# First loads cut and reordered, weight unit 0 in halves, and zero products ahead of the first layer

## The reference, cut

```python
def rms_norm(x, gain, eps=RMS_EPS):
    xf = x.astype(F32)
    y = xf * lax.rsqrt(jnp.mean(xf * xf, axis=-1, keepdims=True) + eps)
    return (y * gain.astype(F32)).astype(x.dtype)

def swiglu_ffn(x, w_in, w_out):
    gate, up = jnp.split(x @ w_in, 2, axis=-1)
    return (jax.nn.silu(gate) * up) @ w_out
...
    h = x
    for l in range(DEPTH):
        h = h + 0.5 * swiglu_ffn(rms_norm(h, ffn1_norm[l]), ffn1_w_in[l], ffn1_w_out[l])
```

## Time and profile before

| what | us |
| --- | --- |
| median of 3 runs | 1832.42 |
| the 3 runs | 1832.42, 1837.83, 1830.93 |
| span of the profiled execution, first to last instruction | 1826.6 |
| PE busy in it | 1796.0 |
| first real product starts at | 10.33 |
| token sums (L464) start at | 18.64 |

### The profile page before, as it was taken

How to read it: one execution, slowest core, us unless ns; L and a number is a source line. 1 busy time by engine, 2 the same in 40 slices (tenths; PEclk the granted TensorE clock), 3 DMA queues, 4 the chain that set the end, 5 groups by cost and what they waited for, 6 DMA issues and landing times.

```text
span 1826.6 us, 35749 instructions
## 1 busy us (share of the span) xinstructions
PE 1796.0 (98%) x15302; PEld 1712.2 (94%) x15302; DVE 1242.0 (68%) x1895; ACT 979.4 (54%) x1493; POOL 68.0 (4%) x32
## 2 busy tenths in 40 slices
PE   7999999999999999999999999999999999999999
PEld 7999998899999999999988999999989889989989
DVE  6775576765767567755767657775766678766676
ACT  6544567355644455445673645445556565556562
POOL 0000011500000000000115000000000000000000
PEclk9999999999999999999999999999999999999999
DMA  8566543233565655565433335665456435446332
GB/s 330 194 196 195 175 150 116 93 128 116 193 191 195 219 190 193 195 196 173 143 112 105 128 119 182 196 196 191 156 162 208 134 109 175 160 147 223 128 114 96
DMA packets 84462, 302.41 MB, mean 166 GB/s; under 512 B 9168, under 2 KB 11728, under 8 KB 84176
## 3 DMA queue, kind: packets, MB, share of 16 engines
q1 hardware_dynamic: 84304, 300.13, 50.0%
HBM read 299.04 MB, written 1.05 MB: 164 GB/s over the span
## 4 chain that ended last, share of the span: by engine, by line
PE 89%; DVE 6%; ACT 4%; issue 1%; DMA 0%; SPq 0%; DVEq 0%; ACTq 0%
PE bank L383 22%; PE bank L390 22%; PE bank L388 22%; PE bank L692 2%; DVE w_lo L1560 2%; PE bank L408 1%; PE bank L407 1%; PE bank L404 1%; PE bank L619 1%; PE bank L1009 1%; PE bank L1060 1%; PE bank L894 1%; PE bank L1030 1%; PE bank L623 1%; PE bank L622 1%
## 5 line engine op out<-in xcount | busy, mean ns | idle before, releaser
L1560 DVE TENSOR_TENSOR w_lo<-ring,w_hi 128x1024 fp32r<-128x1024 f32 x560 | 678.6, 1247 | 93.9 <-ACT w_hi L1126 92.8
L1126 ACT ACTIVATE w_hi<-ring 128x1024 fp32r<-128x1024 f32 x560 | 580.9, 1055 | 245.9 <-PE bank L383 206.2
L383 PE MATMUL bank<-xs,w_hi 128*128 128x256 f32 x2448 | 687.4, 281 | 0.0
L388 PE MATMUL bank<-xs,w_hi 128*128 128x256 f32 (+1 forms) x2454 | 678.4, 277 | 0.0
L390 PE MATMUL bank<-xs,w_lo 128*128 128x256 f32 x2448 | 678.3, 277 | 0.0
L388 PEld LDWEIGHTS bank<-xs,w_hi 128*128 128x128 f32 x2454 | 461.4, 188 | 3.1 <-issue 2.9
L383 PEld LDWEIGHTS bank<-xs,w_hi 128*128 128x128 f32 x2448 | 460.6, 188 | 4.1 <-issue 2.7
L390 PEld LDWEIGHTS bank<-xs,w_lo 128*128 128x128 f32 x2448 | 461.0, 188 | 0.0
L383 PE MATMUL bank<-a,w_hi 128*128 128x256 f32 x704 | 194.3, 276 | 0.0
L388 PE MATMUL bank<-a,w_hi 128*128 128x256 f32 x704 | 194.3, 276 | 0.0
L390 PE MATMUL bank<-a,w_lo 128*128 128x256 f32 x704 | 194.3, 276 | 0.0
(11 more groups left out here) (399 smaller groups left out, 3081.5 us busy)
## 6 DMA issues: line engine op xcount, KB each, us to landing
ring<-in_w SPq DMA_DIRECT2D x560, 512.0 KB, 3.4
arena<-in_mem SPq DMA_DIRECT2D x2, 1024.0 KB, 12.8
const<-in_const SPq DMA_DIRECT2D x1, 1395.0 KB, 15.9
h<-in_x SPq DMA_DIRECT2D x1, 768.0 KB, 7.7
out<-h SPq DMA_DIRECT2D x3, 256.0 KB, 2.5
dec_par<-in_dec SPq DMA_DIRECT2D x1, 615.0 KB, 19.7
h<-in_x SPq DMA_DIRECT2D x1, 256.0 KB, 4.3
out<-h SPq DMA_DIRECT2D x2, 128.0 KB, 2.0
```

What stands on the lines that cost most here:

```text
L383: last = nc.tensor.matmul(o, wh, hi(x, k0 + k), start=k == 0, stop=False, skip_group_check=True)
L388: nc.tensor.matmul(o[:, c:c + piece], wh, lo(x, k0 + k)[:, c:c + piece], start=False, stop=False, skip_group_check=True)
L1126: nc.scalar.activation(w_hi[:, s * UNIT:(s + 1) * UNIT], ring[:, u % RU, :], AF.Copy).then_inc(sems("w_hi"), 1)
L1560: nc.vector.tensor_tensor(w_lo[:, r * UNIT:(r + 1) * UNIT], ring[:, r, :], w_hi[:, s * UNIT:(s + 1) * UNIT].bitcast(F32), ALU.subtract).th ...
```

## The change

1. The gains of the first norm are put in front of `x` in the input, 8 numbers per partition. One load brings the gains and `h` tiles 0-1. `h` is now a view 32 bytes into the tensor `hg`, and a pad of 24 numbers puts `xs` and `arena` back to their offsets modulo 128 bytes.
2. Unit 0 is loaded in two halves of 256 KB, ACT and DVE split each half on its own, and PE may begin with the first four blocks when the first half is split (`half_lo`).
3. `h` tiles 2-7 come in two loads (2-4 and 5-7), and `enc_par` moves from the front of the queue to behind unit 3. It now counts on `loaded_rest`, which is waited for with 64 in place of 48.
4. PE multiplies zeros three times (128x512, plain fp32) into a bank that isn't in use yet, after DVE has written the zeros.

```diff
+        hg = sb("h", KD + KD * T)
+        h = hg[:, KD:KD + KD * T].rearrange("p (a b) -> p a b", a=KD)
+        gain0 = hg[:, 0:KD]
+        sb("pad0", 24)
...
+                if u == 0 and pos == 0:
+                    self.w.e.wait_ge(sems("half_lo"), 1)
+                elif pos == 0 or (u == 0 and pos == UB // 2):
                     self.low_ready(u)
...
-            e.dma_start(enc_par[:, :, :], arrays["enc"]).then_inc(sems("loaded"), 16)
-            e.dma_start(h[:, 0:2, :], arrays["x"][:, 0:2, :]).then_inc(sems("loaded"), 16)
-            e.dma_start(ring[:, 0, :], arrays["w"][0]).then_inc(sems("landed0"), 16)
-            e.dma_start(h[:, 2:KD, :], arrays["x"][:, 2:KD, :]).then_inc(sems("loaded_x"), 16)
+            e.dma_start(hg[:, 0:KD + 2 * T], arrays["x"][:, 0:KD + 2 * T]).then_inc(sems("loaded"), 16)
+            e.dma_start(ring[:, 0, 0:UNIT // 2], arrays["w"][0][:, 0:UNIT // 2]).then_inc(sems("landed_half"), 16)
+            e.dma_start(ring[:, 0, UNIT // 2:UNIT], arrays["w"][0][:, UNIT // 2:UNIT]).then_inc(sems("landed0"), 16)
...
+            e.wait_ge(sems("zeros"), 1)
+            for _ in range(3):
+                nc.tensor.matmul(bank[7][:, :], arena[:, 0:P], arena[:, 0:2 * T], start=True, stop=True,
+                    skip_group_check=True)
```

More of the change, by code:

```diff
@@ L200, in build_program @@
         const = sb("const", CONST.n)
-        h = sb("h", KD, T)
+        hg = sb("h", KD + KD * T)
+        h = hg[:, KD:KD + KD * T].rearrange("p (a b) -> p a b", a=KD)
+        gain0 = hg[:, 0:KD]
+        sb("pad0", 24)
         xs_at = here()
@@ L365, in two @@
                 assert pos + wide <= UB
-                if pos == 0:
+                if u == 0 and pos == 0:
+                    self.w.e.wait_ge(sems("half_lo"), 1)
+                elif pos == 0 or (u == 0 and pos == UB // 2):
                     self.low_ready(u)
@@ L475, in _ @@
             sp = Worker(e, "sp", sems, counts)
-            e.dma_start(enc_par[:, :, :], arrays["enc"]).then_inc(sems("loaded"), 16)
-            e.dma_start(h[:, 0:2, :], arrays["x"][:, 0:2, :]).then_inc(sems("loaded"), 16)
-            e.dma_start(ring[:, 0, :], arrays["w"][0]).then_inc(sems("landed0"), 16)
-            e.dma_start(h[:, 2:KD, :], arrays["x"][:, 2:KD, :]).then_inc(sems("loaded_x"), 16)
+            e.dma_start(hg[:, 0:KD + 2 * T], arrays["x"][:, 0:KD + 2 * T]).then_inc(sems("loaded"), 16)
+            e.dma_start(ring[:, 0, 0:UNIT // 2], arrays["w"][0][:, 0:UNIT // 2]).then_inc(sems("landed_half"), 16)
+            e.dma_start(ring[:, 0, UNIT // 2:UNIT], arrays["w"][0][:, UNIT // 2:UNIT]).then_inc(sems("landed0"), 16)
+            e.dma_start(h[:, 2:5, :], arrays["x"][:, KD + 2 * T:KD + 5 * T]).then_inc(sems("loaded_x"), 16)
+            e.dma_start(h[:, 5:KD, :], arrays["x"][:, KD + 5 * T:KD + KD * T]).then_inc(sems("loaded_y"), 16)
             e.dma_start(ring[:, 1, :], arrays["w"][1]).then_inc(sems("landed1"), 16)
@@ L483, in _ @@
                 e.dma_start(ring[:, u, :], arrays["w"][u]).then_inc(sems(f"landed{u}"), 16)
+                if u == 3:
+                    e.dma_start(enc_par[:, :, :], arrays["enc"]).then_inc(sems("loaded_rest"), 16)
             for dst, src in ((const[:, FIRST:], arrays["const"][:, FIRST:]), (mf[:, :, 1, :], arrays["mem"]),
@@ L511, in mixer_pe @@
             with pe.scope("mix"):
-                pe.e.wait_ge(sems("loaded_rest"), 48)
+                pe.e.wait_ge(sems("loaded_rest"), 64)
                 first_pair(pe, w, xs, 0, "qk_full")
@@ L1166, in memory_high @@
             if f == 6:
-                a.e.wait_ge(*((sems("mem_again"), 16) if l else (sems("loaded_rest"), 48)))
+                a.e.wait_ge(*((sems("mem_again"), 16) if l else (sems("loaded_rest"), 64)))
             if 6 <= f < 10:
@@ L1195, in mixer_act @@
             with a.scope("mix"):
-                a.e.wait_ge(sems("loaded_rest"), 48)
+                a.e.wait_ge(sems("loaded_rest"), 64)
                 s.ahead(u0 + U_MIX + 2)
@@ L1520, in _ @@
             par = [enc_par[:, l, :] for l in range(LAYERS)]
[L1521 to L1529, removed]
+            e.wait_ge(sems("loaded"), 16)
+            for k in range(KD):
+                if k in (2, 5):
+                    e.wait_ge(sems("loaded_x" if k == 2 else "loaded_y"), 16)
+                nc.scalar.activation(hi(xs, k), h[:, k, :], AF.Copy, scale=gain0[:, k:k + 1]).then_inc(*a.tell('x_hi'))
+                if k == 0:
+                    e.wait_ge(sems("landed_half"), 16)
+                    nc.scalar.activation(w_hi[:, 0:UNIT // 2], ring[:, 0, 0:UNIT // 2],
+                        AF.Copy).then_inc(sems("half_hi"), 1)
+                if k == 1:
+                    e.wait_ge(sems("landed0"), 16)
+                    nc.scalar.activation(w_hi[:, UNIT // 2:UNIT], ring[:, 0, UNIT // 2:UNIT],
+                        AF.Copy).then_inc(sems("w_hi"), 1)
+                    s.u = 1
+                if k == 5:
+                    s.highs(2)
+            s.highs(3)
             for j in range(4):
@@ L1663, in mixer_dve @@
             with d.scope("mix"):
-                d.e.wait_ge(sems("loaded_rest"), 48)
+                d.e.wait_ge(sems("loaded_rest"), 64)
                 wf = tiles(ENC(par, 'wab'), KD)
@@ L2070, in _ @@
             s = Lows(d)
+            nc.vector.memset(arena[:, 0:2 * T], 0.0).then_inc(sems("zeros"), 1)
             par = [enc_par[:, l, :] for l in range(LAYERS)]
             for k in range(KD):
-                low_part(d, xs, ENC(par[0], "g_ffn1"), k)
-                if k in (1, 5):
-                    s.lows(1 + k // 4)
+                low_part(d, xs, gain0, k)
+                if k == 0:
+                    d.e.wait_ge(sems("half_hi"), 1)
+                    nc.vector.tensor_tensor(w_lo[:, 0:UNIT // 2], ring[:, 0, 0:UNIT // 2],
+                        w_hi[:, 0:UNIT // 2].bitcast(F32), ALU.subtract).then_inc(sems("half_lo"), 1)
+                if k == 1:
+                    d.e.wait_ge(sems("w_hi"), 1)
+                    nc.vector.tensor_tensor(w_lo[:, UNIT // 2:UNIT], ring[:, 0, UNIT // 2:UNIT],
+                        w_hi[:, UNIT // 2:UNIT].bitcast(F32), ALU.subtract).then_inc(sems("w_lo"), 1)
+                    s.u = 1
+                if k == 5:
+                    s.lows(2)
             s.lows(3)
@@ L2104, in _ @@
                     with g.scope("mix"):
-                        g.e.wait_ge(sems("loaded_rest"), 48)
+                        g.e.wait_ge(sems("loaded_rest"), 64)
                         g.e.wait_ge(*g.need('x_lo', 0))
@@ L2323, in lay_out @@
     feat = lambda x: x[0].T.reshape(KD, P, T).transpose(1, 0, 2)
-    return {"x": feat(i["x"]), "mem": feat(i["mem"]), "const": constants(i["final_norm"]),
+    return {"x": np.concatenate([per_feature(i["ffn1_norm"][0]), feat(i["x"]).reshape(P, KD * T)], 1), "mem": feat(i["mem"]), "const": constants(i["final_norm"]),
             "enc": np.stack(enc, 1), "dec": np.stack(dec, 1), "w": w}
```

## The result

The changed kernel takes 1870.81 us (median of 5 runs, 1866.01 to 1872.06) against 1832.42. The ratio is 1.0199, with a 95% interval of 1.0178 to 1.0219. Forecast were 1831.7 in a range of 1828.8 to 1835.2, so the prediction was wrong by 39 us. Its profiled execution took 1872.06 us around a span of 1870.3.

What follows compares the result with a forecast made beforehand. PE, busy 1796.0 of 1826.6 us, bounds the kernel; at the start it waits for the sums of squares. These come 0.72 us earlier by unit 1's earlier landing: 1832.4 - 0.7 = 1831.7, range 1828.8 to 1835.2.

Steps and rivals of the forecast that it cites:

- The path at the start: Start: load of h 2-7, four ACT tiles, unit 1's high part, DVE's chain and the sums bound it, not PE's first product.
- PE's own gain: First pair at the start: up to 2.6 us, not paid out but turned into a wait for ssum of some 2 us.
- The size at the start: Sums of squares at the start: ssum ends at 17.78 in place of 18.50, 0.72 us earlier.
- The term of the loads: Loads ahead of unit 1: 161 KB less, 0.41 us; ACT begins unit 1 at 10.70 in place of 11.42.
- the good bound's case: Queue's slow start, 3 to 5 us: without that hole 1.4 us more, so the gain would be 2.1 us.
- the middle: Landing of unit 1: the value taken between the good and bad sides, a gain of 0.72 us.
- Rival 3: Behind the sums: the clock falls in PE's new wait, price 1.5 us, giving 1833.2; chance 0.13.
- the wait at 1421: Late in the earlier trace: a 1.8 us wait with the clock staying at 1.00, taken as the nearer row against a fall.
- The zeros: PE's head: three zero products take 3.8 us at half speed, end by 5.0, delay nothing.
- Rival 4: First pair: zeros don't warm anything, it ends at 18.1, gain 0.35 us, 1832.1; chance inside the forecast's 0.60.
- h moved by 32 bytes: ACT and DVE reads of h start at another offset, xs and arena keep theirs modulo 128; nothing put for it.
- something that I don't see: Anywhere in the kernel: the remainder for unnamed causes, no size given; chance 0.02.

Runs made afterwards that it cites:

- e11: The changed kernel with a pad of 56 numbers in place of 24, so xs and arena lie 256 bytes further than before the change; 1831.81 us, ratio 1.0003.
- e12: The changed kernel with a pad of 56 numbers in place of 24 and without the zero products; 1830.16 us, ratio 0.9987.
- e4: The changed kernel at the old addresses, with the first gains loaded by a small load of their own; 1831.45 us, ratio 0.9998.
- e3: The kernel before with only the addresses of the changed one, same loads and instructions; 1868.88 us, ratio 1.021.
- e6: The kernel before with 128 bytes of pad ahead of arena alone; 1850.61 us, ratio 1.0099.
- e8: The kernel before with rst and a 96-byte pad moved ahead of xs: xs and ssum 128 bytes further, arena kept; 1862.89 us, ratio 1.0173.
- e7: The kernel before with 256 bytes of pad behind h, xs to arena all 256 bytes further; 1831.23 us, ratio 1.0001.

## Why the prediction was wrong

- **The path at the start.** Right: load, ACT's tiles, unit 1, DVE's chain, sums. PE's own gain did turn into a wait, of 1.88 us in place of a short one.
- **The size at the start.** The term of the loads was too small. The sums came 1.46 us earlier (1.24 in e11, 1.79 in e12, 0.57 in e4 with one load more), against 0.72. ACT began unit 1 at 9.94 and not at 10.70. The slow start of the queue shrank, which was the good bound's case: the stretch 3 to 5 us moved 202 GB/s where the earlier trace rows had 103. By my estimate that is 0.20 MB, or 0.5 of these 0.76 us at 400 GB/s. The rest is open, and so is the rule: e4 moved 295 GB/s there and began unit 1 only at 10.83. So the value lay between the middle and the bound of 2.1. A microsecond can't be told in medians of runs that scatter over 10 us.
- **Rival 3.** It came true in the profile of the changed kernel, at its price: 3.4 us at half clock. I had trusted the wait at 1421, after which the clock stayed up, and given the fall 0.13.
- **The zeros.** Each plain fp32 product of 512 columns appears as two records 0.85 us apart at half clock, 5.5 us for three. I had taken 3.8 from the row of the sums. They delayed nothing even so: the first real product started at 6.81, as in e12 without zeros. Rival 4 fell, since the products behind them were fast, and it would have changed nothing.
- **The step that failed** is "h moved by 32 bytes ... I put nothing for it". It argued from ACT and DVE, whose time indeed didn't change, and took it for granted that keeping `xs` and `arena` modulo 128 keeps PE's time. The 32 bytes of `h` cost nothing (e11 has them, at ratio 1.0003); the pad behind them moved `xs` and `arena` by 128 bytes against the weights, and that cost 37.6 us (e3 against 1831.28). No row shows a period of 128. The trace did show that equal products run at two paces at a granted clock of 1.00, in the kernel before already (two stretches of it):

```profile
1301.60:1306.80 5.20, 5.20 (x46) 5.20 (x45) 3.26 (x5) 4.23 (x6) 0.00 (x0) 1.00 0.55 176
1309.40:1313.90 4.50, 4.50 (x42) 4.50 (x42) 2.93 (x6) 3.48 (x5) 0.00 (x0) 1.00 0.60 175
```

With the records at the edges taken off these are 118 and 113 ns. Times the 10042 products that ran fast before, 4.5 ns are 45 us at most, which was the rival to price: the pads, the assertions and the odd cut at `f == 1` all pointed at an effect of this kind. The 0.02 left for "something that I don't see", and a range of 6 us, were too little for a change that moves every activation that PE reads.

## What to carry to other kernels

A change to the allocation is a change to every matrix product: keep the distance between the two operands of a product, here weights and activations (modulo 256 bytes in this case), and compare the count of products per 100 us of full PE in both traces before reading anything else. Where PE is the bound over the whole run, 4.5 ns per product are worth more than all that the start can give. An earlier start pays only if what PE waits for next is earlier as well.

## What the runs showed of the hardware

- Streams of fp32r products with 256 columns, a weight load before each, run at 113.0 or 117.5 ns at a granted clock of 1.00. At distance 192 and 64 both paces occur, in the same code and at the same addresses, and one is held over more than a thousand products (3612 from 484.9 to 918.0 us in the changed kernel) until other products or a wait break the stream, or until the operand passes to another distance (e6, e8). At distance 0 the stretch of 500 to 600 us is at 119.6, at 128 at 118.3.
- The pace may also be what scatters the runs. In the profile of e7, at the good distance, the stretch 40 to 120 us was at 117 ns, with 681 products where the kernel before had 708:

```profile
40.00:120.00 80.00, 80.00 (x681) 80.00 (x680) 57.78 (x95) 40.08 (x55) 0.00 (x0) 1.00 0.57 186
```

  The some 1600 products between the first sums and 206 us are slow there; at 4.5 ns they are 7 us, and the profiled span is 5.9 us longer than in the kernel before. Runs of the kernel before at 1838 to 1840 against 1831 fit that; the runs without a profile don't show it.
- Open: why the distance matters. Every product of the streams reads either `w_hi` or `w_lo`, and both moved together in all runs, so which of the two counts wasn't tried. Why the same distance allows both paces, and why a short product can switch between them, is open as well. Not tried was a distance that isn't a multiple of 64, or a cut behind further breaks of the stream, which might lift the slow stretches left at distance 192.
